# Four norm steps, differential rows combined late, and weight halves made behind copy and maximum, in a transformer kernel on one core

## The reference

```python
h = _rms(x, g_attn_pre[l]) * (1.0 + sc_a) + sh_a          # also for the context, with its own sc, sh
q_a, kv_a, dq, dk, dv, gq, gk, gv = jnp.split(h @ w_in, idx, axis=-1)
# MLA: 4 heads of 64 + 32, through low-rank norms
q = (_rms(q_a, g_mla_q) @ w_mla_qb); k_pe = _rope(kv_a[..., 128:]); kv = (_rms(c_kv, g_mla_kv) @ w_mla_kvb)
# differential: 4 heads with two maps each; od is softmax(q k) v of either map
d = od[:, :, 0] - lam * od[:, :, 1]
d = _rms(d, g_diff_sub) * (1.0 - lam_init)
# grouped query: 8 query heads and 2 key heads of 64
q_g = _rope(_rms(gq, g_gqa_q), rope_large); k_g = _rope(_rms(gk, g_gqa_k), rope_large)
```

## Time and profile before

| what | value |
|---|---|
| time, median of 3 runs | 2424.91 us (2424.83 to 2428.48) |
| profiled execution | 2427.63 us |
| its span | 2425.9 us |
| TensorE busy | 2186.5 us, 90% |
| VectorE busy | 1729.5 us, 71% |
| ScalarE busy | 1141.7 us, 47% |
| GpSimd busy | 63.7 us, 3% |
| mean granted clock of TensorE | 0.953 of full speed |

### The profile page before, as it was taken

How to read it: one execution, slowest core, us unless ns; L and a number is a source line. 1 busy time by engine, 2 the same in 40 slices (tenths; PEclk the granted TensorE clock), 3 DMA queues, 4 the chain that set the end, 5 groups by cost and what they waited for, 6 DMA issues and landing times.

```text
span 2425.9 us, 37881 instructions
## 1 busy us (share of the span) xinstructions
PE 2186.5 (90%) x14634; PEld 1963.7 (81%) x14634; DVE 1729.5 (71%) x3415; ACT 1141.7 (47%) x1935; POOL 63.7 (3%) x79
## 2 busy tenths in 40 slices
PE   3998799999999999989987979799989988797998
PEld 3987799999987778879865656799979978567997
DVE  5667679889977877788866566577776665665554
ACT  2543354545554444444444445544454445354444
POOL 1000000000000000000011000000000000000000
PEclk9999999999999999999988889899999998898999
DMA  7648646664468887777741110477767753103664
GB/s 286 204 139 280 203 142 197 217 195 150 144 199 269 263 261 246 272 236 238 249 107 40 53 52 18 148 251 251 246 209 255 255 162 119 53 1 122 186 187 131
DMA packets 139218, 438.73 MB, mean 181 GB/s; under 512 B 15712, under 2 KB 38496, under 8 KB 138528
## 3 DMA queue, kind: packets, MB, share of 16 engines
q1 hardware_dynamic: 109440, 396.93, 51.2%
q10 hardware_dynamic: 25776, 23.97, 2.9%
q0 software_dynamic: 3824, 15.40, 1.8%
HBM read 422.58 MB, written 13.66 MB: 180 GB/s over the span
## 4 chain that ended last, share of the span: by engine, by line
PE 49%; DVE 14%; issue 11%; DMA 9%; ACT 4%; POOL 1%; ACTq 0%; DVEq 0%; POOLq 0%; SPq 0%
PE bk L1718 46%; DVE SPL L1129 4%; DMA RAW<-in_peer 4%; DMA TMP<-kept 3%; PE bk L1724 3%; ACT SPL L787 2%; DVE RAW L1163 1%; DVE R L1129 1%; DVE TMP L1129 1%; DVE ST L1144 1%; ACT R L789 1%; DMA HID<-kept 1%; DVE R L1138 1%; DVE EXT L1163 1%; POOL ST L664 1%
## 5 line engine op out<-in xcount | busy, mean ns | idle before, releaser
L1129 DVE TENSOR_TENSOR SPL<-RAW,SPL 128x1024 fp32r<-128x1024 f32 (+1 forms) x614 | 744.3, 1218 | 365.7 <-ACT SPL L787 364.4
L787 ACT ACTIVATE SPL<-RAW 128x1024 fp32r<-128x1024 f32 (+1 forms) x614 | 644.8, 1054 | 623.2 <-PE bk L1718 275.7
L1718 PE MATMUL bk<-HH,SPL 128*128 128x256 f32 x3840 | 747.9, 288 | 27.5 <-DVE HL L1129 13.7
L1718 PEld LDWEIGHTS bk<-HH,SPL 128*128 128x128 f32 x3840 | 621.0, 194 | 36.4 <-DVE HL L1129 14.3
L1718 PE MATMUL bk<-SPL,WHL 128*128 128x512 f32 x2328 | 555.2, 392 | 13.6 <-DVE WHL L1129 9.4
L1718 PE MATMUL bk<-HL,SPL 128*128 128x256 f32 x1920 | 547.3, 285 | 0.0
L1718 PEld LDWEIGHTS bk<-SPL,WHL 128*128 128x128 f32 x2328 | 429.5, 188 | 107.2 <-issue 19.4
L1718 PEld LDWEIGHTS bk<-HL,SPL 128*128 128x128 f32 x1920 | 372.7, 194 | 2.2
L1718 PE MATMUL bk<-SPL,HH 128*128 128x256 f32 (+1 forms) x1664 | 317.7, 293 | 31.1 <-DVE SPL L1129 19.3
L1718 PEld LDWEIGHTS bk<-SPL,HH 128*128 128x128 f32 x1664 | 271.0, 200 | 40.5 <-issue 26.3
L787 ACT ACTIVATE R<-bk 128x512 f32<-128x512 f32 (+4 forms) x344 | 168.1, 500 | 200.8 <-PE bk L1718 175.9
(11 more groups left out here) (130 smaller groups left out, 1953.3 us busy)
## 6 DMA issues: line engine op xcount, KB each, us to landing
RAW<-in_peer SPq DMA_DIRECT2D x256, 512.0 KB, 4.7
RAW<-in_ada SPq DMA_DIRECT2D x144, 512.0 KB, 4.7
RAW<-in_ffn SPq DMA_DIRECT2D x132, 512.0 KB, 4.2
RAW<-in_win SPq DMA_DIRECT2D x96, 512.0 KB, 4.7
RAW<-in_ffd SPq DMA_DIRECT2D x66, 512.0 KB, 4.3
RAW<-in_wout SPq DMA_DIRECT2D x32, 512.0 KB, 4.8
kept<-TMP ACTq DMA_DIRECT2D x88, 128.0 KB, 3.0
TMP<-kept ACTq DMA_DIRECT2D x66, 128.0 KB, 5.5
```

Source lines behind the costliest of these rows:

```text
L787: ins = e.activation(out, in_, func, bias=bias, scale=scale)
L1129: e.tensor_tensor(out, a, b, op).then_inc(*dve.up(*points))
L1718: ins = e.matmul(out, lhsT, rhs, start=start, stop=stop, skip_group_check=True)
```

## The change

Three parts, and a small one.

1. `gn` becomes four steps: gn_a (squares, sums, mean), gn_b (Newton step, scaling, gains), gn_c and gn_d (two halves of the rotation; gn_d also the key copies). In `qkv_diff_first`, the order of all three stages, the projections come as 7, 4, 5, 6, 0 instead of 7, 0, 4, 5, 6; scl q stands behind pj 0, kpe behind it, and the transposes of qa last.
2. Differential rows: a row with u = 0 is left unscaled; its partner is scaled by lambda times its own reciprocal sum times the first row's sum and added. The values are multiplied as for the other heads, into features by tokens; ScalarE copies them (`ad`), TensorE transposes them back (`dq`), and `df_a` multiplies by the first rows' reciprocal sums while it copies.
3. For the 18 projections in WOVEN, both engines make parts ahead of the step only as far as its first tile asks. ScalarE makes those of the second behind the step's copy, VectorE behind the maximum of the next score row.
4. At the start, VectorE makes no low part ahead of the first `A1` (the first modulation).

In the diff the first loop over PLAN is ScalarE's and the second VectorE's; the piece that waits for "p" is VectorE's `nm`, the one with `cp(d` its `df_a`.

```diff
-    rest = [("pj", l, s, 7), ("pj", l, s, 0), ("scl", l, s, "k"), ("scl", l, s, "q")]
-    rest += [("pj", l, s, 4), ("lr1", l, s, "k"), ("pj", l, s, 5), ("lr2", l, s, "k", 0), ("lr2", l, s, "k", 1), ("kpe", l, s)]
-    rest += [("lr1", l, s, "q"), ("pj", l, s, 6), ("gn", l, s)]
-    rest += [("tr", l, s, "ka", i) for i in range(2)] + [("lr2", l, s, "q", i) for i in range(2)] + [("qpe", l, s)]
-    return first, rest + [("tr", l, s, n, i) for n in ("qa", "kk", "pg") for i in range(2)]
+    rest = [("pj", l, s, 7), ("pj", l, s, 4), ("scl", l, s, "k"), ("pj", l, s, 5), ("lr1", l, s, "k"), ("pj", l, s, 6)]
+    rest += [("lr2", l, s, "k", i) for i in range(2)] + [("gn_a", l, s), ("pj", l, s, 0), ("scl", l, s, "q"), ("kpe", l, s)]
+    rest += [("gn_b", l, s)] + [("tr", l, s, "ka", i) for i in range(2)] + [("lr1", l, s, "q"), ("gn_c", l, s)]
+    rest += [("lr2", l, s, "q", i) for i in range(2)] + [("gn_d", l, s), ("qpe", l, s)]
+    return first, rest + [("tr", l, s, n, i) for n in ("kk", "pg", "qa") for i in range(2)]
...
-        if 8 <= n < 48 and UNITS[n - 8][2:] == (1, 1) and UNITS[n - 8][0] != 1 and UNITS[n - 8][1] % 2:
-            out.append(("ao", l, s, head_of(n - 8) // 2 - 2))
-        out += [("df_a", l, s)] * (n == 24) + [("df_b", l, s)] * (n == 27) + [("dT", l, s)] * (n == 30)
+        if 8 <= n < 48 and UNITS[n - 8][2:] == (1, 1) and UNITS[n - 8][1] % 2:
+            out.append(("ad" if UNITS[n - 8][0] == 1 else "ao", l, s, head_of(n - 8) // 2 - 2))
+        out += [("dq", l, s)] * (n == 24) + [("df_a", l, s)] * (n == 25) + [("df_b", l, s)] * (n == 28) + [("dT", l, s)] * (n == 31)
...
+WOVEN = {("pj",) + a for a in [(0, 1, j) for j in (0, 4, 5, 6, 7)] + [(0, 0, j) for j in range(8)] + [(1, 0, j) for j in (0, 4, 5, 6, 7)]}
...
             for step in PLAN:
+                later = CHUNKS[step][1:] if step in WOVEN else []
+                done = prepare(CHUNKS[step][:1] if later else CHUNKS[step], done)
                 act.stage = STAGE.get(step[0], "layer")
                 if step[0] in steps:
                     steps[step[0]](*step[1:])
+                done = prepare(later, done)
...
             for step in PLAN:
+                now = CHUNKS[step]
+                if step[0] == "ada" and now[0] < SPLITS[0]:
+                    now = [min(now[0], SPLITS[0] - LEAD - 1)]
...
+                if step in WOVEN:
+                    now, later = now[:1], now[1:]
+                done = prepare(now, done)
...
+                if step[0] == "as":
+                    done, later = prepare(later, done), []
...
                 dve.wait_ge(T.at("p", l, s, n))
+                if kind == 1 and u == 0:
+                    return
                 e.reciprocal(r, r).then_inc(*dve.up())
-                if kind == 1 and u == 1:
+                if kind == 1:
                     dve.wait_ge(dve.own, T.at("lam"))
-                    tt(r, r, lamc[:, l:l + 1], ALU.mult)
+                    stt(r, r, lamc[:, l:l + 1], q["RS"][:, n - 1:n], ALU.mult, ALU.mult)
                     dve.wait_ge(dve.own)
                     stt(p, p, r, row(l, s, n - 1), ALU.mult, ALU.add, ("nm", l, s, n))
...
-                cp(d, v2(ps(*key), 2), ("out", key))
+                e.reciprocal(stat(144, 8, s), first).then_inc(*dve.up())
+                dve.wait_ge(T.at("full", key), dve.own)
+                tt(d.rearrange("p i (h d) -> p i h d", d=64), v2(ps(*key), 2).rearrange("p i (h d) -> p i h d", d=64), by_tile,
+                   ALU.mult, ("out", key))
...
+            def dq(l, s):
+                key, d = ("avd", l, s), v2(QS[(l, s)]["Yf"], 2)
+                b = take(key, SCORE[(l, s)])
+                pe.wait_ge(T.at("out", ("av", l, s, -1)))
+                blocks(b, [d[:, k, i * P:(i + 1) * P] for i in range(2) for k in range(2)], P, ("full", key))
```

More of the change, by code:

```diff
@@ L144, in qkv_steps @@
     out += [("pj", l, s, j) for j in ((4, 5, 6) if full else (6,))]
-    out += [("lr1", l, s, "k"), ("lr2", l, s, "k", 0), ("lr2", l, s, "k", 1), ("kpe", l, s), ("gn", l, s)]
+    out += [("lr1", l, s, "k"), ("lr2", l, s, "k", 0), ("lr2", l, s, "k", 1), ("kpe", l, s)]
+    out += [(n, l, s) for n in ("gn_a", "gn_b", "gn_c", "gn_d")]
     out += [("tr", l, s, "ka", i) for i in range(2)] + [("pj", l, s, 3)]
@@ L1063, in ao, with ad @@
                 A(H[s][0][:, block_of(p), :], ps(*key)[:, 0:256], ACT.Copy, ("turned",) + key)
+            def ad(l, s, p):
+                key = ("av", l, s, p)
+                act.wait_ge(T.at("full", key))
+                A(v2(QS[(l, s)]["Yf"], 2)[:, p + 2, :], ps(*key)[:, 0:256], ACT.Copy, ("out", key))
             def dT(l, s):
@@ L1557, in gn, with gn_b @@
                 mean_eps(ss, 64, "gn", l, s)
+            def gn_b(l, s):
+                hd, nh, ss, r, y = heads(l, s)
                 newton(r, y, ss, "gn", l, s)
@@ L1683, in vector_program, with prepare @@
                      "pick": pick, "oh": oh_, "pm": pm, "ph": ph, "fz": fz, "lam": lam, "peer_out": peer_out, "scl": scl, "lr2": lr2,
[L1684 removed]
+                     "kpe": kpe, "gn_a": gn_a, "gn_b": gn_b, "gn_c": gn_c, "gn_d": gn_d, "qpe": qpe, "rd": rd, "as": as_, "nm": nm, "ao": ao, "df_a": df_a, "df_b": df_b, "dT": dT, "op": op,
                      "an_a": an_a, "an_b": an_b, "fs": fs, "fo": fo}
[L1686 to L1697 removed]
+            done, later = 0, []
+            def prepare(chunks, done):
+                upto = min(max([done] + [lead(n) for n in chunks]), len(ORDER))
+                for n in range(done, upto):
+                    if IS_SPLIT[n]:
+                        split_lo(n)
+                    else:
+                        times_c(n)
+                return upto
+            for step in PLAN:
+                now = CHUNKS[step]
+                if step[0] == "ada" and now[0] < SPLITS[0]:
+                    now = [min(now[0], SPLITS[0] - LEAD - 1)]
+                if step[0] == "pe":
+                    now = CHUNKS[("pe", step[1], 0)] if step[2] == 2 else []
+                if step in WOVEN:
+                    now, later = now[:1], now[1:]
+                done = prepare(now, done)
                 dve.stage = STAGE.get(step[0], "layer")
@@ L1983, in av @@
                 pe.wait_ge(T.at("out", ("at", l, s, n)))
-                if g < 4:
-                    key = ("avd", l, s)
-                    b = take(key, VALUE[(l, s)][:1]) if g == 0 else ps(*key)
-                    for i in range(2):
-                        for k, v in enumerate(vals):
-                            end = i == 1 and k == last
-                            done = [("pv", l, s, g)] + [("full", key)] * (g == 3)
-                            mm(b[:, i * 256 + 64 * g:i * 256 + 64 * g + 64], pt[:, k, i * P:(i + 1) * P], v, k == 0,
-                               k == last, *(done if end else ()))
-                    return
                 key = ("av", l, s, g // 2 - 2)
-                b = ps(*key) if g % 2 else take(key, VALUE[(l, s)][::-1])
+                b = ps(*key) if g % 2 else take(key, VALUE[(l, s)][:1] if g < 4 else VALUE[(l, s)][::-1])
                 r = slice(64 * (g % 2), 64 * (g % 2) + 64)
```

71 lines of the change are left out of this document (38 added, 33 removed).

## The result

The changed kernel takes 2434.45 us (median of 7 runs, 2430.45 to 2437.91), the kernel before beside it on the same chip 2426.33 us (7 runs). The ratio is 1.0034, 95% interval 1.0022 to 1.0046: slower, by a little over the 0.2% that can be told from nothing. The forecast was 2431.9. The profiled execution took 2434.45 us with a span of 2432.4.

What follows compares the result with a forecast made beforehand. TensorE, busy 90% of the span, was taken as the bound, so changes pay where it idles or its clock is low. 0.4 + 4.2 + 1.2 + 1.2 = +7.0 us on the median 2424.91 gave 2431.9; range 2413 to 2441.

Steps and rivals of the forecast that it cites:

- start: First projection waits for low parts behind the gate copy, beyond ScalarE's saved idle time: +0.4 us, from -1 to +1.
- context stage: Context rows: low half for the tokens' next projection comes later, among other costs; +4.2 us, from 0 to +8.
- layer-0 tokens: -1.1 us before last projection's end, +1.3 to row 16, +1.0 for differential rows: +1.2, from -4.3 to +3.8.
- layer-1 tokens: Same walk as for the other layer's token stage: +1.2 us, from -4.3 to +3.8.
- the price of the weight halves: Eighteen woven projections: matmuls cover the second tile's late halves, so 0 us; 1.2 us a projection if cover failed.
- The rival for this part: Cover fails and TensorE waits for second tiles, eighteen times 1.2: 22 us, 2446 us; called unlikely, no separate chance.
- The wait that moved: After the last projection, TensorE idles 8.9 us before the ka transposes and 2.5 before kk, instead of 15.23 before qa.
- rival (a): The forecast: wait moves from tr qa to tr ka and the clock falls at it; 2427 to 2439 us, 48%.
- rival (b): Clock returns to 1.00 at once, row 16 starts under 33 us after last projection: 2410 to 2416 us, 22%.
- Ahead of T0: Before the last projection's end: lr1 q gone and rows 6 and 7 adjacent, 1.1 us won; 1.24 us wait stays.
- Differential rows: In each 512-key token stage, four dq transposes and slower value products on TensorE: 1.0 us lost.
- The up to 1.5 us a stage: GpSimd's power and VectorE's low parts exclude each other on SBUF ports: up to 1.5 us more a stage.

Runs made afterwards that it cites:

- kpe moved: Changed kernel without its weight halves part, kpe put back ahead of gn_a: 2407.74 us, 0.9930 of the kernel before.

## Why the prediction was right in its number and wrong in part of its reasons

The number, its range and its side of the 0.2% bound held, the number by luck, since most of its terms did not hold. These are the terms, from the context's projection 7 on, against the traces, one per kernel (so the context's split is good to some 4 us):

| term | forecast | after less before | from what |
|---|---|---|---|
| start | +0.4 | nothing (0.9999 alone) | |
| context stage | +4.2 (0 to +8) | +10.3 | weight halves +7.7, the other parts +2.6 |
| layer-0 tokens | +1.2 | -1.1 | a -3.6, b -0.1, c +2.6 |
| layer-1 tokens | +1.2 | -3.1 | a -5.1, b -0.1, c +2.1 |

**The step that failed** is the price of the weight halves: "I price this part at zero there; if the cover failed it would cost 1.2 a projection". For the token stages, of which it speaks, the zero held in the changed kernel; for the context's rows from 16 on the sum has no price for it at all. The reasoning behind it, that TensorE doesn't wait for the second tile, is right in the changed kernel: no wait for a low part stands inside a projection. (With the part alone one does, 2.13 us.) But the half took a place on two other engines, behind the matmuls in place of beside them, and there it delays the next rows' maxima and exponentials. The prediction saw one of these shifts ("these and what VectorE queues behind them start 1.05 later") and did not carry it on to rows 16 to 39 of the context, where three token projections stand among rows that TensorE waits for. The rival for this part named a failure (a wait for second tiles) that the changed kernel doesn't have. Measured, the part costs 9 us in the changed kernel and 16 alone.

**The wait that moved** was forecast rightly, as mechanism and in size: 8.71 and 2.56 us against 8.9 and 2.5; scl q ends 8.9 us behind T0 (9.2), kpe 11.5 (11.7). So was rival (a)'s clock: 13.6 us at 0.50 that begin 1.1 us into the first wait, and 10.2 behind the second. gn_d ends at 25.4, the 22.5 of the prediction with its 3 us of low clock; the items it lists (3.75, 2.45, the maximum and 3.0 from 11.7 on) give 21.7, and what it leaves unnamed is that VectorE waits for row 14. From there to row 16 it took 8.1 us, 1.3 over the 6.8 at full clock where 2.5 had been added for the second low stretch; but half of the 4.6 us that this stretch reaches past row 16 is lost too, 2.3 us (0.9 in the kernel before), and the sum had no term for that. Row 16 came at 33.5, not 34.8, between the forecast and rival (b)'s bound of 33. With kpe moved it came at 28.2: this wait is what ate the gain of the norm steps in b.

**Ahead of T0** I had 1.1 us won and it was 3.6 and 5.1. The 1.24 us wait shrank by 0.5, since nm 0 is gone, and low stretches went: 3.4 us from 1388.7 in layer 0 and 6.8 from 2054.3 in layer 1, where half of the time was lost, so about 1.7 and 3.4 us (an estimate). I had left the clock out ahead of T0. What starts such a stretch isn't shown by the wait alone: the norm steps alone keep 1.24 us and have none, the differential rows alone have 0.73 us and 6.8 us at 0.50 behind it.

**Differential rows**: 1.0 us was forecast between row 16 and the output projection, 1.1 and 0.8 measured alone. The rest of c, 1.5 and 1.3 us, is the low stretch's longer tail behind row 16. Alone they are even.

**The context stage without the weight halves** cost 4.0 us in context 1 (forecast about 3) and gave 1.4 back in context 2. The 4.0 are two misses of opposite sign: up to the end of the stage's last projection 2.0 us were won (forecast even), and from there to the tokens' first projection it is 34.3 us where before had 28.3, 6.0 more (forecast 3.0). The ka wait is 5.7 us there, not 7.2, and one of 4.6 stands ahead of it.

**GpSimd beside VectorE.** The power of 20 columns took 3.53 us before while VectorE idled. In the changed kernel it took 3.54, and a low part ran over its last us; with kpe moved it took 4.44, and a low part had started 0.17 us ahead of it:

```profile
1422.49 3.54 POOL L667 TENSOR_TENSOR ST<-ST,cons 128x20 f32<-128x20 f32 x1 [20.14 <-DVE ST L1149]
```

```profile
1424.99 1.23 DVE L1143 TENSOR_TENSOR SPL<-RAW,SPL 128x1024 fp32r<-128x1024 f32 x1 [1.79 <-ACT SPL L790]
```

```profile
1412.27 4.44 POOL L667 TENSOR_TENSOR ST<-ST,cons 128x20 f32<-128x20 f32 x1 [23.54 <-DVE ST L1149]
```

It lies beside the last projection's end and nothing waits for its 0.9 us. The same 4.44 stands in every kernel whose low part starts just ahead of the power, the norm steps alone among them, with one low part beside it or two. By the Trainium skill, SBUF — State Buffer, in the section "SBUF: two separate sides", whichever instruction is first gets the shared port pair for its whole length and the other blocks fully. For the power the traces agree nearly: it takes 0.91 us more, and of the low part's 1.22 us 1.05 were left when it began. For VectorE they don't: the low part that began 2.5 us into the power took 1.23 us, and it is 1.22 elsewhere. The up to 1.5 us a stage that the prediction drew from the rule are not seen in the time.

So the total came near by luck, by errors that cancel: 7.7 us too little for the halves, against 6.6 too much in the token stages and 1.6 too much for the rest of the context.

## What to carry to other kernels

Work taken off an engine's queue ahead of a wait is not free where it lands. Ask not only whether its consumer is late, but whether the engine idles at the old place (here 7 to 8 us beside a projection) and what queues behind the new one. Where a block is split so that its parts fit between other work, check each step that was moved along with it: kpe needed an old result only, and standing behind a new one it put 8.7 us of wait on TensorE; moving it, with what moved along, gave 17 us in one company; with the norm steps alone only 0.9981 became 0.9967, some 3 us. Where a program merges the lists, compare the order that comes out as well: a step less in one list moved another by one place, for some 3 us. Measure each part alone, and the whole without it: here two of them, worth -5 and +16 us alone, stood in a change worth +8; taking the second out gave 9 back, not 16.

## What the runs showed of the hardware

The clock is a large part of every term: the context's rows from 1298 on take 65.7 us at a mean of 0.98 and 77.4 at 0.81 with nearly the same matmuls. TensorE ran at 0.50 for 23.9 us of which it was busy 22.9, and single waits from 0.7 to 1.2 us were followed by stretches at 0.50 in some kernels and not in others. What decides it stays open. Two kernels with the same orders on TensorE, ScalarE and VectorE throughout context 2 took 70.8 us at 0.86 and 66.6 at 0.95. GpSimd's power of 20 columns took 4.44 us, not 3.53, whenever a VectorE subtraction with two inputs in SBUF had started 0.17 us ahead of it; a subtraction that started 2.5 us into the power took 1.23 us against 1.22.
